# Attention with one or two copies of each head's bias row, on one Trainium2 core

## The reference, cut to what matters

```python
def forgetting_attention(q, k, v, log_f):
    c = jnp.cumsum(log_f, axis=1).transpose(0, 2, 1)
    for qb in range(S // Q_BLOCK):
        lo, hi = qb * Q_BLOCK, (qb + 1) * Q_BLOCK
        s = jnp.einsum('bqhd,bkhd->bhqk', q[:, lo:hi], k[:, :hi]) * scale
        s = s + c[:, :, lo:hi, None] - c[:, :, None, :hi]
        causal = jnp.arange(hi)[None, :] <= (lo + jnp.arange(Q_BLOCK))[:, None]
        s = jnp.where(causal, s, -jnp.inf)
        p = jax.nn.softmax(s, axis=-1)
        outs.append(jnp.einsum('bhqk,bkhd->bqhd', p, v[:, :hi]))
```

## Time and profile before

| | |
|---|---|
| median of three runs | 1771.4 us (1769.74 to 1771.95) |
| the profiled execution | 1769.39 us, of it span 1767.7 us |
| PE busy | 1660.0 us, 94% of the span |
| DVE busy | 1203.1 us, 68% |
| ACT busy | 887.8 us, 50% |
| POOL busy | 143.1 us, 8% |
| DMA | 390.58 MB, 221 GB/s on average |

### The profile page before, as it was taken

How to read it: one execution, slowest core, us unless ns; L and a number is a source line. 1 busy time by engine, 2 the same in 40 slices (tenths; PEclk the granted TensorE clock), 3 DMA queues, 4 the chain that set the end, 5 groups by cost and what they waited for, 6 DMA issues and landing times. The chain is left out here.

```text
span 1767.7 us, 22853 instructions
## 1 busy us (share of the span) xinstructions
PE 1660.0 (94%) x8336; PEld 1327.3 (75%) x8336; DVE 1203.1 (68%) x1441; ACT 887.8 (50%) x996; POOL 143.1 (8%) x187
## 2 busy tenths in 40 slices
PE   6999999999999999989989999699999999999990
PEld 5888888888888897878868798566677777777660
DVE  5877776643644662277764425789988888888876
ACT  5343343333455341065651102367787878787862
POOL 1000000000000000021100000100000000010115
PEclk9999999999999999999999999799999999999995
DMA  4254453342323233567762231499999999999977
GB/s 168 84 165 157 155 175 99 101 137 88 95 82 90 80 111 105 202 217 242 238 215 101 104 103 49 163 387 392 398 392 398 391 399 391 400 392 399 398 305 267
DMA packets 181078, 390.58 MB, mean 221 GB/s; under 512 B 15680, under 2 KB 91600, under 8 KB 179984
## 3 DMA queue, kind: packets, MB, share of 16 engines
q1 hardware_dynamic: 166880, 330.62, 51.6%
q0 software_dynamic: 8384, 29.63, 5.4%
q10 hardware_dynamic: 5744, 29.40, 4.5%
HBM read 322.15 MB, written 67.46 MB: 220 GB/s over the span
## 5 line engine op out<-in xcount | busy, mean ns | idle before, releaser
L1911 DVE TENSOR_TENSOR e_l<-e_raw,e_h 128x2048 fp32r<-128x2048 f32 x192 | 439.2, 2290 | 64.5 <-ACT e_h L1905 64.0
L1905 ACT ACTIVATE e_h<-e_raw 128x2048 fp32r<-128x2048 f32 x192 | 367.9, 1917 | 88.7 <-PE ps L1940 42.2
L1927 PE MATMUL ps<-e_h,e_xth 128*96 128x512 f32 x512 | 205.2, 401 | 5.1 <-DVE e_l L1911 3.0
L1927 PE MATMUL ps<-e_h,e_xtl 128*96 128x512 f32 x512 | 202.7, 396 | 0.0
L1927 PE MATMUL ps<-e_l,e_xth 128*96 128x512 f32 x512 | 201.8, 394 | 0.0
L218 PE MATMUL ps<-uh,w_h 128*128 128x512 f32 x512 | 162.1, 393 | 9.1 <-DVE ul L1210 4.8
L218 PE MATMUL ps<-ul,w_h 128*128 128x512 f32 x512 | 161.9, 392 | 0.0
L218 PE MATMUL ps<-uh,w_l 128*128 128x512 f32 x512 | 161.3, 391 | 0.0
L218 PEld LDWEIGHTS ps<-uh,w_h 128*128 128x128 f32 x512 | 96.8, 189 | 30.0 <-issue 9.8
L1927 PEld LDWEIGHTS ps<-e_h,e_xth 128*96 128x96 f32 x512 | 83.0, 162 | 45.2 <-issue 7.3
L218 PEld LDWEIGHTS ps<-ul,w_h 128*128 128x128 f32 x512 | 97.0, 190 | 20.4
(11 more groups left out here) (686 smaller groups left out, 3417.0 us busy)
## 6 DMA issues: line engine op xcount, KB each, us to landing
e_raw<-w_exp_gate SPq DMA_DIRECT2D x64, 1024.0 KB, 21.0
e_raw<-w_exp_up SPq DMA_DIRECT2D x64, 1024.0 KB, 21.0
e_raw<-w_exp_down SPq DMA_DIRECT2D x64, 1024.0 KB, 21.2
wn_raw<-w_in SPq DMA_DIRECT2D x32, 512.0 KB, 5.0
w_raw<-w_in SPq DMA_DIRECT2D x12, 1024.0 KB, 5.4
at_qk<-qk_d ACTq DMA_DIRECT2D x6, 2048.0 KB, 9.4
y_d<-e_y ACTq DMA_DIRECT2D x32, 384.0 KB, 6.4
y_d<-zeros POOLq DMA_DIRECT2D x22, 384.0 KB, 4.0
```

The source lines that it names most:

```text
L1905: act.activation(self.e_h[m % SPLIT][:, :, :], self.e_raw[slot][:, :, :], ACT.Copy).then_inc(self.e_hi[m % SPLIT], 1)
L1911: dve.tensor_tensor(self.e_l[slot][:, :, :], self.e_raw[slot][:, :, :], self.e_h[m % SPLIT][:, :, :].bitcast(F32), ALU.subtract).then_inc( ...
L1927: mm = pe.matmul(ps, x[:, k, :], w[:, k, :], start=first and first_piece, stop=last and last_piece)
```

## The change

The kernel after holds two copies of each head's bias row in SBUF. Blocks with even n use one, those with odd n the other, for the mask and for the sum. The mask of block n now waits until DVE has read block n-2, the last one that used the same copy; the first two blocks of a head wait for the loads instead, and there for both copies (32 in place of 16 on the semaphore). Each bias load is issued twice, one behind the other, into the two copies, at the three places where it was issued once. The mask tile moves to another part of SBUF, to make room for the copies.

```diff
-        self.at_bias = [work.put(f"at_bias{c}", [P, T]) for c in range(2)]
+        self.at_bias = [[work.put(f"at_bias{c}{b}", [P, T]) for b in range(2)] for c in range(2)]
...
     def load_head_bias(self, eng, i, c):
-        eng.dma_start(self.at_bias[c][:, :], self.bias_d[2 * i + c].partition_broadcast(P)).then_inc(self.bias_in[c], 16)
+        for b in range(2):
+            eng.dma_start(self.at_bias[c][b][:, :], self.bias_d[2 * i + c].partition_broadcast(P)).then_inc(self.bias_in[c], 16)
...
-        mask = work.put("at_mask", [P, P])
...
         sb = [(upper if n < NT // 2 else work).put(f"at_s{n}", [P, keys_of(n)]) for n in range(NT)]
+        mask = upper.put("at_mask", [P, P])
...
                 def diagonal(i, n):
                     c = n // NT
-                    block = bias[c][:, block_of(n) * P:(block_of(n) + 1) * P]
-                    if n % NT == 0:
-                        pool.wait_ge(bias_in[c], 16 * (i + 1))
+                    block = bias[c][n % 2][:, block_of(n) * P:(block_of(n) + 1) * P]
+                    if n % NT < 2:
+                        pool.wait_ge(bias_in[c], 32 * (i + 1))
                     else:
-                        pool.wait_ge(least, tiles * i + n)
+                        pool.wait_ge(least, tiles * i + n - 1)
                     pool.tensor_tensor(block, block, mask[:, :], ALU.add).then_inc(masked, 1)
...
-                                                 in1=bias[c][:, 0:keys], scale=1.0, scalar=-NEG, op0=ALU.add,
+                                                 in1=bias[c][n % 2][:, 0:keys], scale=1.0, scalar=-NEG, op0=ALU.add,
```

## The result

The changed kernel took 1778.49 us, median of 20 runs, beside 1772.46 us for the kernel before on the same chip: a ratio of 1.0032, 95% interval 1.0023 to 1.004. By that ratio it is 5.7 us slower; the forecast was 2.3 us, with 1777.8 as the upper end of its range.

A forecast was written before the change was run, and what follows sets the result against it. TensorE was taken to bound the stage, with losses at head starts from head 3 on. Late starts of 3.2 us less head 0's gain of 0.9 made 2.3 us slower than 1771.4: 1773.7 us, range 1770.2 to 1777.8.

The forecast's parts named there:

- what the change removes: Head 0's mask waits: two-ahead masks let ScalarE start sooner, gaining 0.9 us, between 0 and 2.0.
- ScalarE's run: Sign in head 0: ScalarE's unbroken run of work starts near 763.2 in place of 764.08.
- The fourteen waits of later heads: VectorE's mask waits after head 0, 3.4 us: covered by its idle time for TensorE's value products, worth nothing.
- Heads 1 and 2 start early: Starts of heads 1 and 2: their bias loads are early, so the second copy stays hidden and delays nothing.
- how far a second copy lands behind the first: Bias loads of heads 3 to 7: second copy lands 1.27 us after the first, bounds 0.4 and 2.9.
- 418 GB/s: Rate while the bias moves, said to be as fast as any stretch; 512 KB then take 1.25 us.
- second rival: Starts of heads 3 to 7: second copy meets the query and key load at half rate; 5.7 us slower, 1777.1; chance 0.25, shared with full adding up.
- the late starts of heads 3, 5 and 7: First blocks wait for both copies: 0.6 us at head 3, totals of 1.8 by head 5 and 3.0 by head 7.
- the slip of SP's queue: Stores and loads behind the second copy: slip absorbed by the query and key load's pace; 0.1 us taken, bounds 0 to 1.27.
- taken off for slack, and for a later wait in head 3: Head starts have about 0.1 us slack; head 3 also gets 0.6 off for TensorE's later wait of 0.61.
- The sum over heads: Heads 3 to 7: the next head's wait swallows a delay, the head after next inherits it; 3.2 us by head 7.
- stalls of 2 us and more: Sign at the first blocks of heads 3 to 7 that the second copy collides with the query and key load.

The follow-up runs named there:

- g2_after_again: The changed kernel run again, unaltered, on another chip beside the kernel before: ratio 1.0032 (1.0017 to 1.0046).
- the last version: Changed kernel with a semaphore per copy, first load inside the last inverses' round trip, second inside the next head's first inverses' trip: 0.9987, then 0.9981.
- f2_and_wait_both: Changed kernel with the second copy issued behind the store of the next head's first inverses, a head's first block waiting for both copies: ratio 1.0039.
- g1_one_head: Kernel before plus a second, unread bias load in head 3 alone, whose first mask waits for both: one execution, stage end 158.38 us.
- g4_both_in_trips_again: Second run of the changed kernel with a semaphore per copy and each load inside its own inverses' round trip: ratio 0.9981 (0.9969 to 0.9994).

## Why the prediction was wrong, by its own steps

**Right: what the change removes.** The masks two blocks ahead gain head 0 1.02 us (13.94 to 12.92; forecast 0.9), and 1.7 at the full clock, within the bound of 2.0. ScalarE's run begins as forecast near 763.2, where the earlier trace rows had 764.08:

```profile
763.26 0.83 ACT L1450 ACTIVATE at_s<-at_s,at_small 128x640 f32<-128x640 f32 x1 [0.24 <-DVE at_small L1498]
```

The fourteen waits of later heads were covered but for little: head 1 is 0.12 us shorter (18.18 to 18.06), and without any mask heads 1 to 7 together gain 1.1. Heads 1 and 2 start early, as forecast.

**Mostly right: how far a second copy lands behind the first.** Forecast: 1.27 us. Measured in heads 2 to 7 of the changed kernel: 1.2 to 1.6 in ten of twelve cases, 2.4 and 2.0 in heads 3 and 5 of the first profile. Two figures on the way were wrong: 418 GB/s isn't the fastest of that trace (it shows 479 from 813 to 814 us), and a copy 2.9 us late makes 7.1 us by the forecast's own sum, more than the second rival's 5.7.

**The step that failed: the late starts of heads 3, 5 and 7, above all the slip of SP's queue.** The prediction put these starts at 0.6, 1.2 and 1.2 us and all slips at 0.2, 3.2 in all. The stretches ahead of them grew by 9.3 us in the first profile and by 7.7 in the second (`g2_after_again`). Each of these starts comes 0.6 us behind the landing of the last copy, before and after, so the growth can be split by the issues and landings of the bias loads:

| us, heads 3, 5 and 7 together | forecast | first profile | second |
|---|---|---|---|
| bias issued later, counted from the start of the head before | 0.2 | 2.3 | 2.9 |
| first copy takes longer than the one copy before | 0 | 1.4 | 0.9 |
| second copy lands behind the first | 3.8 | 5.7 | 4.0 |
| taken off for slack, and for a later wait in head 3 | -0.8 | 0 | 0 |

Of the 6.1 and 4.5 us by which the sum fell short, the slip is 2.1 and 2.7, the largest part in both. "A slip of 1.27 us is absorbed there", 0.1 taken, was read at head 4's inverses, an issue 14.6 us behind the query and key load. The slip is plainest ahead of head 3, 1.7 and 1.9 us, of which about 1 is that head 2 starts earlier and the queue doesn't follow. The round trip that breaks there is that of head 1's first inverses: it stands behind the bias loads, and goes out as the next head starts, about when the next query and key load does. Asked for 1.8 us ahead of that load (before) they took 3.1 us; asked for 0.4 to 1.6 us behind it, in all five profiles with a second load right behind the first, 8.8 to 9.7. The first inverses of heads 3 and 5 are asked for 0.6 and 5.0 us behind such a load in the first profile and take 8.7 and 7.0; in the second, 2.5 and 2.7 behind, and take 8.4 and 7.3. There the slips are smaller, from -0.2 to 0.9 us. A slow inverse load isn't a loss by itself: in the kernel before with its load moved, those of heads 2, 3 and 4 take 9.0 to 10.8 us. What is shown is that the place on the queue decides whether there is a loss: the changed kernel with its loads moved, the wait for both kept, is at 1.0000 in place of 1.0032, and the load alone, with no first block waiting, at 1.0021.

**The sum over heads: the right form for another reason.** Delays were to be swallowed by the next head's wait and handed to the one after it. One late head shows otherwise: in full, to all. So it is in the changed kernel, whose heads 4 and 6 start 2.9 and 5.7 us late in the first profile; forecast were 1.2 and 2.4. What is swallowed is the next head's own late copy: counted from the late starts of heads 3 and 5, the next bias goes out 2.8 and 1.5 us sooner than before (second profile 2.1 and 1.4), so the queue has caught up. That is why the lumps stand at every second head, as in the forecast's sum; no run took it apart.

The stretches of the first profile grew by -1.02 (head 0), -0.12 (1), +4.14 (2), -0.07 (3), +2.38 (4), +0.42 (5), +2.81 (6) and -0.14 (7), in all +8.4. VectorE's mask waits come to 8.3 too, but they are where the delay shows and not the whole cause: they hold the slip of the queue and the slower copies as well.

**The rival that gave the right number.** "Second copy collides" said 1777.1, 5.7 us more, and 5.7 was measured; its sign, stalls of 2 us and more, came too. Its mechanism is there in part. Where the copy landed 2.4 and 2.0 us behind the first (heads 3 and 5 of the first profile; half the rate would make it 2.5), the query and key load had been issued 4.3 and 3.5 us before that landing; with one late head it was 3.3 us and 5.8. In heads 3 and 5 of the second profile that load had been issued 3.2 us before and the copies land 1.4 behind, and the stage is as long (162.18), so the collision adds to the loss where it happens and isn't what makes it. That the rival's figure came out is luck. The collision is plainest in the last version: a copy issued 0.74 us ahead of the 2 MB load took 10.4 us, as long as that load (10.3) and longer than half the rate would make it (an estimate from the 5.1 us of the earlier trace rows and 1.25 us more: some 6 us). By the Trainium skill, DMA: Bandwidth & Descriptors, section Queues, rings and completion order, an engine takes a packet from each queue in turn. That run agrees in that the two share; it doesn't show the turns.

Measured against the 1771.4 us on which the forecast stood, a ratio of 1.0032 is that rival's 1777.1; the kernel before was 1.1 us slower in these runs.

**What was left out.** No term stood for the clock. Where it fell in the two profiles of the changed kernel, the head's first value product came 1.2 to 1.6 us later than at the full clock. How much of that reaches the stage's end isn't shown.

## What to carry to other kernels

A load on a queue with a written order is paid for by what stands behind it as well: before adding one, follow the next round trip on that queue, and see whether it still gets out ahead of the next big load. Let each buffer's first reader wait for that buffer alone; one count for two loads makes the first block wait for bytes that only the second reads, and that alone was 0.0023 and 0.0032 in two pairs here. An idle engine in a wait of the same queue (here SP, within the inverses' trip) was the place where such loads cost least here. A copy that goes out just ahead of a big load of another queue can still be late there (10.4 us).

## What was not expected of the hardware

TensorE's clock fell to 1.2 GHz inside the stage, for 3 to 7 us, in the changed kernel and in four others, and in the profile of the kernel before in no head from 1 to 7. The length of its idle time doesn't tell when. It fell within or behind idle times of 3.28 us (after, head 3), 2.15, 2.22 and 2.04 (after again, heads 3, 5 and 7), 4.05, 4.72 and 4.98 us (`f2_and_wait_both`, `g1_one_head`, `g4_both_in_trips_again`), and with the load alone behind 1.29 and 0.28; it didn't behind 2.50 and 2.11 (after, heads 5 and 7) or 2.54 us (`f2_and_wait_both`, head 6). Where it falls for some 3 us, the head's first value product comes 1.2 to 1.6 us later, and the same kernel showed it once in one execution and three times in another.

A store of 2 KB took from 1.4 to 9.7 us, by what was ahead of it on its queue or moving beside it.
